# The sparse layer's gates by tanh with fill in eighths, and the mixers' scores of two blocks put together

## What is computed

```
# sparse layer: 8 heads of 128, 2 key heads, top 128 keys of each query by an index score
q, k, v, gate, qi, ki, wi = split_cols(hn @ w_in, ODD_SPLITS)
att = dsa_attention(rms_norm(q), rms_norm(k), v, qi, ki, wi, rel_bias)   # softmax over chosen keys
return (att * jax.nn.silu(gate)) @ w_out

# mixer, 12 heads of 64 (layer 0 with a decay between tokens, layer 1 with strided windows)
sc = einsum('bhqd,bhkd->bhqk', q_block, k) * scale + c[query] - c[key]    # decay in layer 0 only
p = softmax(where(key <= query, sc, NEG));  o = p @ v
# memory attention, 4 heads of 64 over 256 memory tokens
p = softmax(einsum('bhqd,bhkd->bhqk', qm, km) * 64 ** -0.5);  o = p @ vm
```

## Time and profile before

| | us |
|---|---|
| median of 3 runs | 1773.67 |
| lowest and highest | 1772.76, 1777.25 |
| the profiled execution's own time | 1775.61 |
| its span | 1773.5 |
| TensorE busy | 1737.5 |
| GpSimd busy | 1016.0 |
| VectorE busy | 941.5 |
| ScalarE busy | 541.1 |
| mean granted TensorE clock | 0.995 |

### The profile page before, as it was taken

One profiled execution on the slowest core, in us unless ns is written; L12 is line 12 of the kernel. 1 busy time (PEld: TensorE's weight loads), 2 busy tenths in 40 slices (PEclk: granted clock), 3 DMA queues, 4 the chain that ended last, 5 costly groups with the idle time before them and its releaser, 6 DMA issues.

```text
span 1773.5 us, 24668 instructions
## 1 busy us (share of the span) xinstructions
PE 1737.5 (98%) x9668; PEld 1408.1 (79%) x9668; DVE 941.5 (53%) x1898; ACT 541.1 (31%) x1196; POOL 1016.0 (57%) x1046
## 2 busy tenths in 40 slices
PE   7998999999999999999999999999999999999998
PEld 6886678787669977779888888888777888888887
DVE  6896634794543364433663166336765356415642
ACT  3624533312532344423210011125664321101111
POOL 7533456563327753345777677757344577677762
PEclk9999999999999999999999999999999999999999
DMA  5321223221223322113432333222211233233331
GB/s 179 108 79 42 96 78 101 72 84 45 67 97 108 95 72 72 49 48 90 115 93 89 99 97 101 97 88 80 71 48 48 72 107 116 87 96 95 96 101 53
DMA packets 174195, 152.16 MB, mean 86 GB/s; under 512 B 5448, under 2 KB 149192, under 8 KB 174080
## 3 DMA queue, kind: packets, MB, share of 16 engines
q1 hardware_dynamic: 172480, 149.10, 27.5%
q10 hardware_dynamic: 1600, 1.48, 0.3%
HBM read 147.38 MB, written 2.14 MB: 84 GB/s over the span
## 4 chain that ended last, share of the span: by engine, by line
PE 93%; DVE 4%; ACT 1%; issue 1%; DMA 1%; SPq 0%; DVEq 0%
PE ps L282 78%; PE ps L2103 3%; PE ps L2121 2%; PE ps L2136 2%; PE ps L1613 1%; PE ps L353 1%; PE ps L1591 1%; PE ps L2109 1%; PE ps L1528 1%; DMA h<-x 1%; PE ps L1549 1%; PE ps L1537 0%; DVE ps L1280 0%; PE ps L1603 0%; PE ps L735 0%
## 5 line engine op out<-in xcount | busy, mean ns | idle before, releaser
L127 POOL TENSOR_SCALAR w_hi<-w_raw 128x512 fp32r<-128x512 f32 x520 | 317.6, 638 | 715.2 <-PE ps L282 710.0
L131 POOL TENSOR_TENSOR w_lo<-w_raw,w_hi 128x512 fp32r<-128x512 f32 x520 | 693.6, 1366 | 11.4
L282 PE MATMUL ps<-x_hi,w_hi 128*128 128x512 f32 (+2 forms) x1432 | 534.4, 373 | 1.7 <-DVE x_lo L548 1.7
L282 PE MATMUL ps<-x_hi,w_lo 128*128 128x512 f32 (+2 forms) x1432 | 524.0, 366 | 0.0
L282 PE MATMUL ps<-x_lo,w_hi 128*128 128x512 f32 (+2 forms) x1432 | 523.9, 366 | 0.0
L282 PEld LDWEIGHTS ps<-x_hi,w_hi 128*128 128x128 f32 (+1 forms) x1432 | 270.8, 189 | 63.9 <-issue 16.5
L282 PEld LDWEIGHTS ps<-x_hi,w_lo 128*128 128x128 f32 (+1 forms) x1432 | 270.9, 189 | 44.3
L282 PEld LDWEIGHTS ps<-x_lo,w_hi 128*128 128x128 f32 (+1 forms) x1432 | 271.3, 189 | 40.7
L2416 DVE SCALAR_TENSOR_TENSOR ffn_cv<-ps,col,ffn_cv 128x510 f32<-128x510 f32 (+1 forms) x176 | 131.8, 749 | 192.6 <-ACT ffn_cv L2394 188.0
L2394 ACT ACTIVATE ffn_cv<-ps,col 128x512 f32<-128x512 f32 x88 | 63.8, 776 | 496.6 <-PE ps L282 496.6
L310 DVE TENSOR_TENSOR h<-h,ps 128x512 f32<-128x512 f32 x64 | 43.8, 687 | 255.7 <-PE ps L282 255.6
(11 more groups left out here) (357 smaller groups left out, 2412.2 us busy)
## 6 DMA issues: line engine op xcount, KB each, us to landing
w_raw<-w_up SPq DMA_DIRECT2D x88, 512.0 KB, 5.1
w_raw<-w_down SPq DMA_DIRECT2D x16, 1024.0 KB, 5.0
w_raw<-od_w_in SPq DMA_DIRECT2D x12, 1024.0 KB, 5.2
w_raw<-w_in_fox SPq DMA_DIRECT2D x10, 1024.0 KB, 5.3
w_raw<-w_in_dil SPq DMA_DIRECT2D x10, 1024.0 KB, 5.3
w_raw<-w_out SPq DMA_DIRECT2D x8, 1024.0 KB, 5.0
w_raw<-ev_w_in SPq DMA_DIRECT2D x6, 1024.0 KB, 5.5
w_raw<-w_down SPq DMA_DIRECT2D x8, 768.0 KB, 4.5
```

The source lines that it names most:

```text
L127: ins = pool.tensor_scalar(hi[:, c:min(c + PIECE, size)], raw[:, c:min(c + PIECE, size)], 1.0, 1.0, ALU.mult, ALU.mult)
L131: ins = pool.tensor_tensor(lo[:, c:min(c + PIECE, size)], raw[:, c:min(c + PIECE, size)], hi[:, c:min(c + PIECE, size)].bitcast(F32), ALU. ...
L282: mm = pe.matmul(o, l, r, start=start and i == 0, stop=stop and i == 2)
```

## The change

In the sparse layer:

- Fill is cut into eighths (one k tile, three matmuls), 1, 2, 1, 2 of them at each head's four steps from step 0 on, until the 32 eighths are used up, at step 21.
- Gates 3 to 7 are no longer evacuated with copy or silu. ScalarE writes tanh(x/2) from PSUM into the gate's tile, and VectorE, at the next step, adds 1 and multiplies with x, still in PSUM (`gate`, counted by `gate_read`). The factor 1/2 is put into the product with the values.
- Before the attention ScalarE does one exp of a single column.
- `finish` is cut into `gated` (step with `qb == 2`, counts `freed`), `high` (`qb == 3`) and `low` (the next `qb == 0`, counts `made`).
- An output piece waits for the reading of the gate in its own bank, and for the operand of its own head.

In the mixers, `column` places the second block's scores behind the first one's in the same bank: blocks 0 and 1 of a pair of heads, and each two blocks of a memory pair. One call of `scores` issues both, and the call for the second returns at once. `logits` of the first block waits for the count of the second block's scores.

```
-            FILL = ((1, 2, 3), (1, 2, 3), (1, 2, 3), (1, 2, 3), (1, 2, 3), (0,))
+            FILL = (1, 2, 1, 2)
+                for u in range(self.OUT[0]):
+                    eighths = min(self.FILL[u % T], 4 * KD - n)
+                    self.fill[u] = [(self.gate_unit + 4 + i // KD, i % KD) for i in range(n, n + eighths)]
+                    n += eighths
+                self.ready_at = {m: u for u, pieces in self.fill.items() for m, k in pieces if k == KD - 1}
+                self.ready_at[self.gate_unit + 3] = 0
...
-                        if used:
+                        if used and used[-1] >= self.gate_unit + 3:
+                            pe.wait_ge(self.gate_read, used[-1] - self.gate_unit - 2)
+                        elif used:
                             pe.wait_ge(self.evacuated, used[-1] + 1)
...
+                        if i in (0, 4):
+                            pe.wait_ge(self.gate_read, 4 + i // 4)
                         if i == 0:
-                            pe.wait_ge(self.evacuated, len(self.units))
                             pe.wait_ge(W.split_done, out_.slots[0][0] + 1)
-                            pe.wait_ge(self.freed, 4)
+                        if i < 4:
+                            pe.wait_ge(self.made, i + 1)
...
-                for i in range(4):
+                for i in range(3):
                     evacuate(self.gate_unit + i, self.gate[:, i, :], ACT.Silu)
+                linker(act, act_link)(act.activation(seam_stat[:, 0, 0:1], eps_col[:, 0:1], ACT.Exp))
...
+                def tanh(i):
+                    act.activation(self.gate[:, i, :], self.done(self.gate_unit + i), ACT.Tanh, scale=0.5).then_inc(self.tanh_ready, 1)
...
+                def gate(i):
+                    g = self.gate[:, i, :]
+                    dve.wait_ge(self.tanh_ready, i - 2)
+                    dve.scalar_tensor_tensor(g, g, 1.0, ps[:, self.units[self.gate_unit + i][2], :], ALU.add,
+                                             ALU.mult).then_inc(self.gate_read, 1)
...
+                        dve.wait_ge(self.gate_read, hd - 2)
+                        dve.scalar_tensor_tensor(g, ps[:, 6, :], 0.5, g, ALU.mult, ALU.mult).then_inc(self.freed, 1)
...
+                    for m, ready in self.ready_at.items():
+                        if ready == u - 1:
+                            gate(m - self.gate_unit)
                     if u % T == 2 and u > T:
-                        finish(u // T - 1)
-                finish(CH - 1)
+                        gated(u // T - 1)
+                    if u % T == 3 and u > T:
+                        high(u // T - 1)
+                    if u % T == 0 and u > T:
+                        low(u // T - 2)
...
+            def column(self, p, qb):
+
+                if isinstance(p, str):
+                    return 2 * P * (qb % 2)
+                return P if qb == 1 else 0
...
+                    blocks = (qb, qb + 1) if qb < T - 1 and self.column(p, qb + 1) else (qb,)
+                    for b in blocks:
+                        c, w = self.column(p, b), self.keys(p, b) * P
+                        for e in range(2):
+                            q_, k_, _ = self.head(p, e)
+                            mm = pe.matmul(ps[:, e, c:c + w], q_[:, b * P:(b + 1) * P], k_[:, 0:w], start=b == qb, stop=not decay,
+                                           skip_group_check=True)
...
-                        dve.wait_ge(self.scored.s, self.scored.at(2 * s + e + 1))
+                        shared = qb < T - 1 and self.column(p, qb + 1) > 0
+                        dve.wait_ge(self.scored.s, self.scored.at(2 * (s + shared) + e + 1))
...
-                sp.wait_ge(odd.freed, 1)
+                sp.wait_ge(odd.made, 1)
```

## The result

The changed kernel takes 1757.18 us (median of four runs, 1756.45 to 1758.65); the kernel before, run beside it, 1773.22. The two medians differ by 16.0 us. The ratio of the executions is 0.9902, with a 95% interval of 0.9891 to 0.9914, and by it the change gives 17.4 us (15.2 to 19.3), where 12.6 were forecast. The profiled execution took 1756.76 us, its span is 1754.9.

The account below looks back on a forecast made before the run. TensorE, busy 1737.5 of 1773.5 us, was taken as the bound. Sparse layer 9.3 us plus mixers 3.3 made 12.6 off 1773.67, giving 1761.0 us; range 1756.0 to 1768.0.

Parts of the forecast that it names:

- Put together with the step before, the 0.63 stays: Mixers: joining score steps saves only 0.19 us a pair; a score step's own 0.63 us remains; 3.3 us in all.
- Start of the attention: Sparse layer's first steps: exp table loaded earlier, fill in the hole, less a gate read; 1.6 us gained, bounds 0.6 to 2.4.
- Middle: Third head's values in the attention: no silu table loads left, so the wait before them goes; 2.4 us gained.
- Steps 22 and 23: Attention's last third: of stalls of 0.91 and 1.90 us, cutting `finish` and dropping silu return 2.0 us; bounds 0.8 to 2.8.
- The last two stalls: Attention's last third: stalls of 0.62 and 1.13 us, with `finish` alone before them, shrink by 1.7 us; bounds 1.0 to 1.75.
- The clock: Attention from 490 us: TensorE's clock drop after standstill goes, one head's values take 1.55 us less; bounds 0 to 1.55.
- (a): Mixers: the joined scores save nothing; 9.3 us gained in all, 1764.4 us; chance 0.08.
- (e): Mixers: joined scores delay the first block's logits about 1 us in twenty pairs, TensorE stands still; 1784 us; chance 0.02.
- Rival (b): Mixers: the second block's weight loads are hidden in the joined group; 3.4 us more gained, 1757.7 us; chance 0.05.
- (d): Attention's gates: tanh isn't in exp's table, so five gates cost two loads each, 7.5 us in all; 1768.6 us; chance 0.04.
- (c): Attention: stalls return with gate reads and GpSimd's splits, terms at lower bounds; 6.3 us gained, 1767.4 us; chance 0.10.
- (f): Sparse layer: the change works but the removed stalls reappear at the stage's end; 1770 to 1774 us; chance 0.03.

Follow-up runs that it names:

- f4: The changed kernel plus a one-column silu after the tanh of step 10, so two more table loads in the third head: 1758.25 us, ratio 0.9917.
- i1: The changed kernel with GpSimd's split of one weight slot of the next stage waiting until seven operands are made: 1756.77 us, ratio 0.9897.
- h1: The kernel before with nothing but `finish` cut in three: 1770.05 us, ratio 0.9972.
- e1: The kernel before with only the changed mixers, its sparse layer unchanged: 1765.78 us, ratio 0.9945.
- f1: The changed kernel with `gated`, `high` and `low` together again at the step with `qb == 2`: 1765.52 us, ratio 0.9952.
- f2: The changed kernel with fill in quarters at the steps of before, instead of eighths: 1757.06 us, ratio 0.991.
- e4: The changed kernel with each pair's scores issued head by head, both blocks of one and then of the other: 1756.77 us, ratio 0.9898.

## Why the prediction was right in direction and short in size

**The step that failed** is the one in the mixers: "Put together with the step before, the 0.63 stays". It took the exposed 0.17 us of a score step to belong to its matmuls. The joined group shows it is paid once a group: eight records take 0.86, not 1.05. The term was 3.3 us (0.19 a pair) and measured 7.63 (0.38 a pair). That is more than the upper bound that stood beside it, 7, and its 4.3 us make nearly all of the gap between 12.6 and the 17.4 of the ratio, or the 17.6 of the two traces. The 0.19 from the transposes' end was right. The evidence that decided against the 0.17, that "the alternating heads of one step don't hide them today", was no evidence: the two heads of a step do run side by side (their records start in pairs), and the 0.17 sits at the two ends of the group, behind its first pair and behind its last. The row of 1350.61 gives the group as one line, so it never said what a second step behind the first would pay.

**The first pair.** A net loss of 0.3 us was allowed. The first mixer gained 3.78 us, the second 3.85, so the net loss is small, 0.07 beside the second mixer. The stall that was 0.49 before the second block's scores is 0.35 before the third's.

**Start of the attention**: 1.6 forecast. First scores to first values was 12.18 us before and is 432.51 - 421.39 = 11.12 after, and now holds three more fill matmuls of 0.23: 1.06 + 0.69 = 1.75. The gate read was to cost 0.6; the stall of 0.70 came, with slow scalings in it too. The first transpose comes 2.26 us after the first scores instead of 4.18. That is 1.92 sooner, not 1.28 to 1.8: beside the 1.28 of the table load, the scaling took 0.65 us instead of 1.29 (the sum had 0.25 for it). The total is right by two errors that cancel.

**Middle**: 2.4 forecast, 2.42 gone. f4 shows that the loads by themselves are about half of that.

**Steps 22 and 23**: 2.0 forecast, 2.81 - 1.48 = 1.33 measured, within the bounds but not at the 0.8 of idle time named. "I allow 0.5 for GpSimd's split" was the part that was too small: without the split the stall is 0.71 shorter (i1), because it lengthens the scaling by 0.85, from 0.49 to 1.34. The rest is the queue of gate read and `gated`, with 0.33 us of waiting for the tanh, which the step's sum of 1.5 us did not count.

**The last two stalls**: 1.7 forecast, 1.75 measured, nothing left; h1 shows that the cut alone ends them. **The clock**: 1.55 forecast, and the values do take 1.55 us less. But this is luck in part: e1 shows the same two stalls without a drop behind them and drops worth 3.17 us at two others, so the size of the term belongs to the one execution that was read. What the traces do share: each of the three in which `finish` is whole (before, e1, f1) has a drop in its attention, and none of the eleven in which it is cut has one. h1 is among these with stalls of 2.44 and 2.41, behind which e1's drops stood. How often drops come isn't known, with one trace of each kernel.

**Fill**: 0, and f2 measures 0.11 us against the eighths, as the sum of 0.55 gained in the heads and more than that lost at steps 20 to 24. The terms so measured give 1.75 + 2.42 + 1.33 + 1.75 + 1.55 = 8.80 of the 9.95 us. No term stood for the other 1.15, but the runs place most of it. About 0.55 is the eighths' gain in heads two to five (f2 has these heads as slow as before: 10.23 and 10.20 against 10.20 and 12.74 - 2.42 = 10.32). About 0.4 is in the last two stalls: by starts the cut shortens the two heads by 0.96 and 1.19 us (h1 8.13 and 9.47, e1 9.09 and 10.66), 2.15 where the idle times in the brackets add up to 1.75. So an idle time understates what its stall costs. That the attention's 9.3 came near its 9.95 is thus in part luck, with 0.67 too much at steps 22 and 23 against 1.15 that nobody had counted.

**The signs.** The attention went from 88.96 us to 79.01, not "about 82 instead of 91"; only the difference of 9 fits the forecast's own sum. No load, no stall on `gate_read` or `made`, and the clock at 1.00 from 480 to 515 us came as said.

**The rivals.** (a) and (e) fell with the 7.63 us: TensorE waits for nothing in the mixers beyond the first steps of the first one (one stall of 0.35, before scores). Rival (b)'s 1757.7 is the time nearest to what came, and its place, the entry of the second block's scores, is the right one. The Trainium skill (TensorE: Matmul & The Clock Gate, Part 3: Packing small matmuls) would give it by weights pulled ahead for another row group. The traces agree that this happens: the two heads' records start 0.01 us apart, and in e4 the second head's 128 columns start ahead of the first head's 256, which are issued first. But it happens within a group of before too, so it is not by itself what the joining saves; that is the 0.10 and the 0.09 at the group's two ends. (d) fell: tanh runs behind exp with no load between them, which agrees with what the Trainium skill (ScalarE: Activation LUTs, Table sets) lists. Of (c), the stalls of the gate read (0.70) and of the split came, each smaller than the whole rival. (f) fell: what the attention gained, the stages behind it kept.

## What to carry to other kernels

Put small groups of matmuls of one kind together even where their columns and loads stay the same: each group pays a change of kind and an entry, here 0.19 us each. On a helper engine that others wait for, don't place several operations in the step with the least cover: cutting one block of three in three steps gave 5.9 of the 9.95 us, 4.35 of them without the clock's drop. And before an operation between two SBUF tiles is moved, look what GpSimd does at its new time.

## What the runs showed of the hardware

- A group of 64-row score matmuls behind 128-row transposes pays its entry once, however many matmuls it has and whatever satisfied wait or order of heads is inside (0.86 us in four kernels for the eight records, 1.05 in two groups). The surcharges are 0.10 ahead of it, 0.10 behind its first pair and 0.09 behind its last.
- Matmuls of two heads in different halves of the 128 rows run side by side, their starts 0.01 us apart, and in e4 even those that are not issued next to each other. Full rows run one by one (0.43 us for 512 columns) and make the two mixers 14.9 us longer, in spite of 0.20 a group less in surcharges.
- VectorE's operations from SBUF to SBUF can take 2 to 3 times as long while GpSimd splits weights (scaling of 512 columns 0.49 to 1.34 us, cast 0.42 to 1.15, subtraction 0.69 to 1.63); those that read PSUM don't (0.68 and 0.69 in both). Not each one does: a scaling of 384 columns took 0.42 us at 428.79 in the kernel before, with a split beside it. That agrees with the Trainium skill (SBUF — State Buffer, Who interferes with whom): a cast or a tensor_scalar between SBUF tiles can run in a mode that needs ports which GpSimd holds for a whole instruction, and an operation with two SBUF inputs needs one of them; one with at most one SBUF input outside those modes doesn't. The added 0.73 to 0.94 us are less than one of the split's subtractions takes (5.31 / 4 = 1.33 us).
- A table load takes 1.28 us and the next activation starts right behind it (450.16 + 1.28, next at 451.46, in f4).
- Whether the granted clock falls behind a stall differs between executions of the same code: 0.91 and 1.90 us of standstill were followed by 0.66 in one and by 1.00 in another (e1); the stall of 2.42 by values of 2.42 us in one and of 3.31 in the other; the first stall of 2.44 by full clock in one and by 0.50 in the other. A drop cost 1.49 to 1.68 us each time.
